# A split-precision layer stack: the sum of the gate halves moved ahead of the conditioning rows in three chunks, and the rows spread differently

## What is computed

```python
cond = jax.nn.silu(c)
for l in range(DEPTH):
    mod = (cond @ w_ada[l] + b_ada[l])[:, None, :]
    sh1, sc1, g1, sh2, sc2, g2 = jnp.split(mod, 6, axis=-1)
    ...
    x = layer_norm(ALPHA * x + (1.0 + g1) * y, ln_g[l, 0], ln_b[l, 0])
    u = x * (1.0 + sc2) + sh2
    y = conv_ffn(u, w_up[l], conv_w[l], conv_b[l], w_down[l])
    x = layer_norm(ALPHA * x + (1.0 + g2) * y, ln_g[l, 1], ln_b[l, 1])

def conv_ffn(u, w_up, conv_w, conv_b, w_down):
    h = u @ w_up
    a, g = h[..., :FFN_DIM], h[..., FFN_DIM:]
    gp = jnp.pad(g, ((0, 0), (CONV_WIDTH - 1, 0), (0, 0)))
    gc = conv_b
    for i in range(CONV_WIDTH):
        gc = gc + gp[:, i:i + S_, :] * conv_w[i]
    return (jax.nn.gelu(gc) * a) @ w_down
```

## Time and profile before

| | us |
|---|---|
| median of three runs | 2306.08 (2305.86 to 2310.16) |
| the profiled execution | 2305.81 |
| its span, first to last instruction | 2304.0 |
| PE busy in the span | 2232.0 |
| DVE busy in the span | 1693.7 |
| ACT busy in the span | 1006.8 |

### The profile page before, as it was taken

The page is one execution under the profiler, slowest core; times in us unless marked ns, Lnnn a source line. Parts: engine busy times, 40 slices in busy tenths (PEclk is TensorE's granted clock), DMA queues, the critical chain, the costliest instruction groups (busy, mean ns, idle before and its releaser), DMA issues. The chain is left out here.

```text
span 2304.0 us, 27954 instructions
## 1 busy us (share of the span) xinstructions
PE 2232.0 (97%) x11235; PEld 1864.5 (81%) x11235; DVE 1693.7 (74%) x1668; ACT 1006.8 (44%) x1002; POOL 8.4 (0%) x19
## 2 busy tenths in 40 slices
PE   7899999999999999999999999999999999999996
PEld 3777776788888888888888888888888888888885
DVE  2799899869977777888877767775698655566555
ACT  1445343454443444443355444435544334444432
POOL 1000000000000000000000000000000000000000
PEclk8999999999999999999999999999999999999998
DMA  9999889868878888789877777865688556665553
GB/s 364 363 404 352 295 291 358 301 215 284 297 251 310 304 273 285 266 277 327 324 263 271 272 261 269 288 220 165 221 299 299 194 193 202 193 190 183 196 192 124
DMA packets 392227, 612.66 MB, mean 266 GB/s; under 512 B 21113, under 2 KB 205073, under 8 KB 390562
## 3 DMA queue, kind: packets, MB, share of 16 engines
q1 hardware_dynamic: 389378, 608.42, 75.7%
q10 hardware_dynamic: 2272, 2.20, 0.3%
q0 software_dynamic: 448, 0.25, 0.0%
HBM read 608.70 MB, written 2.10 MB: 265 GB/s over the span
## 5 line engine op out<-in xcount | busy, mean ns | idle before, releaser
L912 DVE TENSOR_TENSOR w_lo<-w_raw,w_hi 128x2048 fp32r<-128x2048 f32 x380 | 847.8, 2233 | 408.8 <-ACT w_hi L579 342.1
L579 ACT ACTIVATE w_hi<-w_raw 128x2048 fp32r<-128x2048 f32 x380 | 710.3, 1870 | 852.8 <-PE banks L1389 515.8
L1503 PE MATMUL banks<-u_hl,w_hi 128*128 128x512 f32 x2368 | 576.6, 392 | 8.7 <-DVE g_sum L1121 6.9
L1503 PEld LDWEIGHTS banks<-u_hl,w_hi 128*128 128x128 f32 x2368 | 432.6, 188 | 96.0 <-DVE g_sum L1121 9.4
L1389 PE MATMUL banks<-w_hi,u_hl 128*128 128x512 f32 x1920 | 477.8, 401 | 12.4 <-ACT u_hl L643 5.3
L1389 PEld LDWEIGHTS banks<-w_hi,u_hl 128*128 128x128 f32 x1920 | 361.7, 192 | 96.2 <-issue 17.1
L1511 PEld LDWEIGHTS banks<-u_hl,w_lo 128*128 128x128 f32 x2368 | 308.6, 191 | 14.5
L1511 PE MATMUL banks<-u_hl,w_lo 128*128 128x256 f32 x2368 | 313.0, 283 | 0.0
L1389 PE MATMUL banks<-w_hi,hid_hi 128*128 128x512 f32 x688 | 269.7, 392 | 0.0
L1389 PE MATMUL banks<-w_hi,hid_lo 128*128 128x512 f32 x688 | 267.8, 389 | 0.0
L928 DVE SCALAR_TENSOR_TENSOR ada_acc<-ada_w,silu_c,ada_acc 128x1024 f32<-128x1024 f32 x187 | 239.2, 1279 | 17.2 <-DMA ada_w<-in_w_ada 10.7
(11 more groups left out here) (213 smaller groups left out, 1252.7 us busy)
## 6 DMA issues: line engine op xcount, KB each, us to landing
ada_w<-in_w_ada SPq DMA_DIRECT2D x352, 512.0 KB, 6.5
w_raw<-in_w_up SPq DMA_DIRECT2D x344, 512.0 KB, 4.7
w_raw<-in_w_down SPq DMA_DIRECT2D x152, 512.0 KB, 4.8
w_raw<-in_w_qkv SPq DMA_DIRECT2D x96, 512.0 KB, 4.7
w_raw<-in_w_in_ab SPq DMA_DIRECT2D x64, 512.0 KB, 8.6
ada_w_more<-in_w_ada SPq DMA_DIRECT2D x32, 512.0 KB, 10.4
w_raw<-in_w_out_ab SPq DMA_DIRECT2D x32, 512.0 KB, 6.2
w_raw<-in_w_o SPq DMA_DIRECT2D x32, 512.0 KB, 5.0
```

What stands on the lines that cost most here:

```text
L579: nc.scalar.activation(whi[:, u % HL_SLOTS, 0:width], raw[:, u % RAW_SLOTS, 0:width], ACT.Copy).then_inc(w_hi, 1)
L912: nc.vector.tensor_tensor(wlo[:, u % HL_SLOTS, 0:width], raw[:, u % RAW_SLOTS, 0:width], whi[:, u % HL_SLOTS, 0:width].bitcast(f32), ALU.s ...
L1503: ins = nc.tensor.matmul(bank[banks[s] + i][:, :], tile(whi, k, s, i), uhl[:, kt].rearrange("p a s -> p (a s)"), start=first and k == 0, s ...
```

## The change

In `steps`, for `up_a` and chunks below 7 (here 4, 5 and 6), `g_add` is issued ahead of `beside`, that is ahead of the row of unit c.2. The rows of pairs 10 and 22 now lie on chunks 4 to 7, with the counts 1, 0, 1, 1 in chunks 4, 5 and 6 and 2, 1, 2, 2 in chunk 7. Those of pairs 11 and 23 begin at chunk 8, with one for each unit in chunks 8 and 9 and two for each of d0 to d3. Pairs 11 and 23 are summed one unit behind their last rows, so behind d4 and d5. Pair 12 (layer 0 only) begins at d6 in place of d3, with 2, 2, 2 and then one row for each unit, and ends at the same unit as before.

Rows for each unit, before and after:

| | chunk 4 | chunk 5 | chunk 6 | chunk 7 | chunk 8 | chunk 9 | d0 to d5 | sums behind |
|---|---|---|---|---|---|---|---|---|
| before | 1 2 1 1 | 2 1 1 2 | 1 1 2 1 | 1 2 1 1 | 2 1 1 2 | 1 1 2 1 | 0 0 0 1 1 1 (layer 0) | 7.1, 7.2; d1, d2 |
| after | 1 0 1 1 | 1 0 1 1 | 1 0 1 1 | 2 1 2 2 | 1 1 1 1 | 1 1 1 1 | 2 2 2 2 0 0 | 8.1, 8.2; d4, d5 |

```diff
     for m, layer in ((10, 0), (22, 1)):
         first = PH[layer, "up_a"]["unit"]
-        fill(m, first + 16, [1, 2, 1] * 4)
-        fill(m + 1, first + 28, [1, 2, 1] * 4)
+        fill(m, first + 16, [1, 0, 1, 1] * 3 + [2, 1, 2, 2])
+        fill(m + 1, first + 32, [1, 1, 1, 1] * 2 + [2, 2, 2, 2])
     first = PH[0, "down_a"]["unit"] + 3
-    for m in range(12, 16):
+    fill(12, first + 3, [2, 2, 2] + [1] * 10)
+    for m in range(13, 16):
         fill(m, first + KT * (m - 12), [1] * KT)
...
     sum_at = {m: s + 2 for m, s in ends.items()}
-    sum_at |= {m: ends[m] + 1 for m in LATE_PAIRS} | {1: 2, 2: 12, 3: 16, 6: 39}
+    sum_at |= {m: ends[m] + 1 for m in LATE_PAIRS + (11, 23)} | {1: 2, 2: 12, 3: 16, 6: 39}
...
                             ln_affine(2 * key[0], AFFINE_AT.index((c, j)))
+                        early = key[1] == "up_a" and c < 7
+                        if j == own and early:
+                            g_add(*key, c)
                         beside(unit_no(key, c, j - 2))
-                        if key[1] in ("up_a", "up_b") and j == own:
+                        if key[1] in ("up_a", "up_b") and j == own and not early:
                             g_add(*key, c)
```

## The result

The changed kernel takes 2313.51 us (median of 12 runs), the kernel before 2307.52 us (12 runs). The ratio is 1.0029, with a 95% interval of 1.0022 to 1.0036: slower, by 6 to 7 us. The profiled execution of the changed kernel took 2312.12 us with a span of 2310.3; before it was 2305.81 and 2304.0. Another measurement of the changed kernel, beside later experiments, gave 1.0028 (1.0018 to 1.0038). The forecast started from 2306.08, the median of the first three runs before; over twelve it is 1.4 us higher.

What follows compares the result with a forecast made beforehand. PE, busy 97%, was taken as the bound, so only its waits pay. Per layer -5.23 + 1.42 + 3.6 = -0.21, both layers -0.4; with one clock fall +1.3, so 2307.4 us, range 2303.0 to 2310.5.

Steps and rivals of the forecast that it cites:

- wait behind d4: At pair 11's sum in the down projection, PE waits for the last row on DVE: 3.6 us per layer.
- late landing: The loads of the last two rows, at median landing 6.7 us, end the last row late: 0.5 us taken.
- the clock: PE's clock falls to half speed behind the long down-projection wait: 1.7 us each, 6 in 10 per layer.
- What bounds, and what the change removes: PE bounds; in chunks 5 to 7 its waits for g_sum and the gate copy go: 5.23 us per layer.
- 1.42 new at chunk 8: Chunk 7's seven rows delay its sum of halves on DVE, so PE waits anew at chunk 8: 1.42 us.
- sum ahead of the row, fewer rows: In chunks 4 to 6, both edits together remove PE's three g_sum waits: 4.32 us per layer.
- bare chain of 3.0 us on DVE: DVE's low halves and rows in d2 to d4 alone make PE wait 3.0 us, some 0.1 to refill.
- Rival B: Last rows of pair 11 land in 8.4 us, PE waits 5.4: 2309.3 to 2312.7 us; 13 in 100.
- gate copy of pair 10: DVE's first gate copy, done at 611.4, asked at 611.85: hidden with 0.4 to spare, else up to 1 us.

Runs made afterwards that it cites:

- e_halfload: The changed kernel with rows 8 to 15 of pairs 11 and 23 loaded by half, 256 KB in place of 512: 2311.90 us, 1.0018.
- e_early: The kernel before with only the sum of halves put ahead of the conditioning row in chunks 4 to 6 of up_a: 2307.21 us, 1.0003.
- e_sum2: The changed kernel with the sums of pairs 11 and 23 two units behind their last rows (d5, d6): 2305.91 us, 1.0000 of the kernel before.
- e_rowsfirst: The changed kernel with loads of rows 12 to 15 of pairs 11 and 23 issued ahead of the same unit's weights: 2310.36 us, 1.0020.
- e_awake: The changed kernel with ten unused matmuls of 256 columns on PE ahead of the first sum of pairs 11 and 23: 2309.00 us, 1.0008.

## Why the prediction was wrong

The forecast was 2307.4 us, +1.3 us and so no difference that the runs can tell, with a range to 2310.5. It was 2313.5, slower by 6.0. The steps that failed are two terms of the wait behind d4: the late landing (0.5, measured 2.0) and the clock (one fall of 1.7, measured two of 1.8 and 2.5). Step by step:

- **What bounds, and what the change removes: right.** Forecast 5.23 us per layer gone and 1.42 new at chunk 8, so 3.81 gained. Measured 3.88: chunk 8 lost 0.94 (25.05 without its 22.29 and two sums of 0.91) and chunk 7 lost 0.41, together 1.35.
- **Which of the two edits brings it: not asked.** I booked 4.32 us for "sum ahead of the row, fewer rows". The experiments give it to the rows alone; the order by itself brings nothing.
- **The new wait behind d4: the place and the chain right, the size wrong.** The bare chain of 3.0 us on DVE came out (3.14 and 2.9 with half loads). The term that failed is the landing of the rows, "I take 0.5". It was 2.0, with landings of 8.3 us. The page gave 4.4 to 8.4 us, and I took a value near the middle for the loads with the most in front of them: issued late because of the slots, behind a unit's weights, in a stretch where the DMA engines are full (1.04 at 408 GB/s in the stretch of the wait). The 0.60 that I set against this was a mean over 29 us of the kernel before, in which these loads were not made. PE stood for 5.21 and 5.03 us where I had 3.6: 3.0 us in both layers.
- **The clock: right that it falls, wrong in how often and how much.** I gave 6 in 10 for each layer and took one fall of 1.7 us. It fell in both layers, in the changed kernel's second profile too, and from the sum to the end of d5 PE took 5.97 and 6.70 us where it takes 4.19 awake: 1.8 and 2.5, so 4.3 in place of 1.7. The 1.7 was half of a stretch of 3.41 us; here the clock was at 0.50 for 6.8 us in each layer, a part of it before PE worked again. The fall didn't need the late rows: it came in both layers of `e_halfload` as well, behind the 3.1 and 2.9 us of the bare chain, and cost 2.8 there. The rule of the Trainium skill against idle gaps between bursts of matmuls (TensorE: Matmul & The Clock Gate, Why this matters for your kernels) agrees with these falls.
- **Rival B was what happened.** It said late rows, 2309.3 us without a fall and 2312.7 with both, and PE waits of 5.4; measured 5.0 and 4.9, and both falls. I gave it 13 in 100, and the range stopped in its middle. With the waits and falls as measured, the same sum gives -5.23 + 1.42 + 5.1 + 2.2 per layer, 3.5, so +7 in all, within 1 us of what was measured.
- **The gate copy of pair 10: right**, no wait in the changed kernel. But it was the next thing in line, as e_early shows with its 3.35 us.

## What to carry to other kernels

When work is moved so that its result is asked for one unit after its last piece, write down the time between the last piece's end and the first that asks, with the load of that piece at the slow end of its landings: it is issued late and stands behind the weights. The same eight rows with the sum two units later (and pair 12 moved back to free the accumulator) turned +0.3% into -0.3%. In `e_early` PE waited less than before (6.7 us for the gate copies, where it was 6.9 for `g_sum` and 1.5 for the copies), but in one piece per layer, with the clock falling behind each, and nothing was gained. While the clock still falls, a shorter wait gives back less than its length: in `e_halfload` 3.9 us less of waiting gave 2.6. And where DVE is busy without a gap, reordering it only moves the wait to the next thing it delivers.

## What the runs showed of the hardware

The granted clock behind PE's waits inside a steady stretch of matmuls: behind 1.8 us followed by 1.2 (e_sum2) it stayed at the 2.4 GHz level; behind 2.9 and 3.1 (e_halfload), 3.3 (e_rowsfirst and e_early), 4.1 (e_rowsfirst) and 5.0 us (the changed kernel) it fell to the 1.2 GHz level. In the earlier trace rows waits of 2.7 and 2.9 us had the fall as well.

The length of the wait alone doesn't decide it. In a stretch where PE has little to do (1.30 us of work in the 4.17 us from 1150.67), the kernel before has a wait of 1.87 us with one more fall behind it, which the prediction didn't count:

```profile
1152.54 1.30 PE L1606 MATMUL banks<-consts,x_tok 128*128 128x128 f32 x8 [1.87 <-DVE x_tok L1076]
```

```profile
1154.84:1158.25 3.41, 3.19 (x8) 2.50 (x9) 3.35 (x6) 1.62 (x4) 0.00 (x0) 0.50 0.00 0
```

The same wait at 1552.4 us has none, and in `e_halfload` the clock stayed at 1.00 behind a wait of 2.99 us at 323.6.

In the changed kernel the clock fell before PE worked again. The two stretches at 0.50:

```profile
666.37:673.20 6.83, 3.75 (x7) 2.35 (x8) 5.43 (x4) 0.00 (x0) 0.00 (x0) 0.50 0.80 306
1820.08:1826.90 6.82, 5.33 (x11) 3.52 (x12) 4.19 (x4) 0.00 (x0) 0.00 (x0) 0.50 0.71 270
```

They are equally long, but PE works for 3.75 us of the first and 5.33 of the second. At half speed that is an estimated loss of 1.9 and 2.7 us, near the 1.8 and 2.5 found above: the more of the low clock lies inside the wait, the less it costs. Matmuls whose results nobody uses kept the clock at 1.00 in both layers of `e_awake`.
